# RMSNorm statistics of a two-layer hybrid block: the pre-norm's sum of squares as columns that are spread back, the post-norm's last squares added by matmul, the residual's coefficient applied on ScalarE

## The reference, cut to what matters

```
def _rmsnorm(x, g):
    y = xf * lax.rsqrt(jnp.mean(xf * xf, axis=-1, keepdims=True) + EPS)
def _pre(x, g, mod, k):
    return _rmsnorm(x, g) * (1.0 + mod[:, 3 * k + 1]) + mod[:, 3 * k]
def _post(x, y, g, mod, k, weight):
    return x + weight * mod[:, 3 * k + 2] * _rmsnorm(y, g)
```

## Time and profile before

| | |
|---|---|
| time, median of 3 runs | 2871.16 us (2861.47 to 2871.52) |
| span of the profiled execution | 2864.4 us |
| TensorE busy | 2680.7 us (94%) |
| VectorE busy | 1677.3 us (59%) |
| ScalarE busy | 716.3 us (25%) |
| mean granted TensorE clock | 0.969 |

### The profile page before, as it was taken

The page is one execution under the profiler, slowest core; times in us unless marked ns, Lnnn a source line. Parts: engine busy times, 40 slices in busy tenths (PEclk is TensorE's granted clock), DMA queues, the critical chain, the costliest instruction groups (busy, mean ns, idle before and its releaser), DMA issues.

```text
span 2864.4 us, 39514 instructions
## 1 busy us (share of the span) xinstructions
PE 2680.7 (94%) x16446; PEld 2496.0 (87%) x16446; DVE 1677.3 (59%) x2235; ACT 716.3 (25%) x977; POOL 821.0 (29%) x1292
## 2 busy tenths in 40 slices
PE   5899999998899889999999799999998898899996
PEld 4899999997869789999999699999998766588885
DVE  5868877865582686766665743343434683644444
ACT  4211121113413421111111322112122413322222
POOL 1258775732050200000000228767551050100001
PEclk9999999999999999999999899999999999899998
DMA  9443444442455134343441232222233455133321
GB/s 314 125 132 125 152 152 128 129 165 87 151 147 162 45 111 125 111 130 114 132 126 52 74 74 87 95 94 89 94 103 120 138 167 161 57 96 99 96 89 59
DMA packets 340459, 337.09 MB, mean 118 GB/s; under 512 B 52529, under 2 KB 311225, under 8 KB 336697
## 3 DMA queue, kind: packets, MB, share of 16 engines
q1 hardware_dynamic: 279224, 204.07, 24.3%
q10 hardware_dynamic: 51840, 77.07, 8.0%
q0 software_dynamic: 9216, 53.42, 5.0%
HBM read 290.02 MB, written 44.50 MB: 117 GB/s over the span
## 4 chain that ended last, share of the span: by engine, by line
PE 81%; DVE 11%; ACT 3%; DMA 2%; issue 2%; SPq 1%; POOL 0%; DVEq 0%; ACTq 0%; POOLq 0%
PE ps L454 71%; DVE adaW L541 3%; PE ps L1390 2%; PE ps L582 2%; PE ps L1089 2%; ACT wH L439 1%; PE ps L1415 1%; DVE tmpN L1168 1%; DMA y_d<-YC 1%; DVE wL L446 1%; DVE rmsX L1177 1%; DVE xT L1049 1%; PE ps L1404 1%; DMA xin<-in_x_dram 1%; PE ps L1074 1%
## 5 line engine op out<-in xcount | busy, mean ns | idle before, releaser
L454 PE MATMUL ps<-hH,wH 128*128 128x384 f32 (+1 forms) x2928 | 1019.9, 348 | 67.9 <-DVE hL L1186 48.1
L454 PE MATMUL ps<-hL,wH 128*128 128x384 f32 (+1 forms) x2928 | 1011.6, 345 | 0.0
L454 PE MATMUL ps<-hH,wL 128*128 128x384 f32 (+1 forms) x2928 | 1010.9, 345 | 0.0
L446 DVE TENSOR_TENSOR wL<-raw,wH 128x1024 fp32r<-128x1024 f32 x300 | 392.0, 1319 | 551.9 <-ACT wH L439 551.3
L454 PEld LDWEIGHTS ps<-hH,wH 128*128 128x128 f32 x2928 | 556.1, 190 | 95.6 <-issue 55.9
L454 PEld LDWEIGHTS ps<-hL,wH 128*128 128x128 f32 x2928 | 556.3, 190 | 18.1
L454 PEld LDWEIGHTS ps<-hH,wL 128*128 128x128 f32 x2928 | 555.5, 190 | 18.5
L454 PE MATMUL ps<-midH,wH 128*128 128x384 f32 (+1 forms) x1232 | 426.2, 346 | 12.7 <-DVE wL L446 9.9
L454 PE MATMUL ps<-midH,wL 128*128 128x384 f32 (+1 forms) x1232 | 423.6, 344 | 0.0
L454 PE MATMUL ps<-midL,wH 128*128 128x384 f32 (+1 forms) x1232 | 423.2, 344 | 0.0
L439 ACT ACTIVATE wH<-raw 128x1024 fp32r<-128x1024 f32 x300 | 310.8, 1050 | 448.2 <-PE ps L454 399.3
(11 more groups left out here) (257 smaller groups left out, 2382.3 us busy)
## 6 DMA issues: line engine op xcount, KB each, us to landing
raw<-in_ffn_gu_dram SPq DMA_DIRECT2D x176, 512.0 KB, 3.8
adaW<-in_w_ada_dram ACTq DMA_DIRECT2D x40, 1536.0 KB, 7.0
raw<-in_ffn_down_dram SPq DMA_DIRECT2D x88, 512.0 KB, 3.7
x_d<-xT POOLq DMA_DIRECT2D x4, 3072.0 KB, 9.6
xT<-x_d POOLq DMA_DIRECT2D x4, 3072.0 KB, 11.1
W_d<-gW POOLq DMA_DIRECT2D x16, 512.0 KB, 4.0
VT_d<-gVT ACTq DMA_DIRECT2D x16, 512.0 KB, 3.0
raw<-in_w_in_dram SPq DMA_DIRECT2D x16, 512.0 KB, 6.2
```

The costliest lines, as they stand in the source:

```text
L446: nc.vector.tensor_tensor(wL[:, n % SPLIT_SLOTS, :], raw[:, n % RAW_SLOTS, :], wH[:, n % SPLIT_SLOTS, :].bitcast(f32), ALU.subtract).then_ ...
L454: ins = nc.tensor.matmul(dst, a, b, start=first and n == 0, stop=last and n == 3 * len(pairs) - 1)
```

## The change

The pre-norm's statistic is made as the post-norm's was: `pre_tensor` takes each chunk's squares as stationary operands, six blocks of 128 tokens, against one column of ones, and accumulates over the eight chunks in six columns; ScalarE takes the root of these six columns and VectorE their reciprocal into `rstd`; TensorE waits for it (`rs_x`) and spreads the columns. `pre_vector` reads the spread from PSUM; `rmsX` is gone. This holds for the start's pre-norm too, inside `pre_tensor`.

In the post-norm chunk 7's squares go to TensorE as six more stationary blocks, instead of being added to `sumY` on VectorE. `coef_post` moves ahead of the last `down` (or of `add_half`). ScalarE multiplies `yT` by `coefP` in place, chunk m - 1 after squaring chunk m, in two instructions for the two streams; chunks 6 and 7 both come after the last square. VectorE's normalisation is then one plain multiplication of 768 tokens without a coefficient.

```
+    def stat_columns(pe, at, squares, tok0, first, last):
         for b in range(tok0 // 128, TOK // 128):
+            ins = nc.tensor.matmul(at[:, b:b + 1], squares[:, b * 128:(b + 1) * 128], ones[:, 0:1],
+                                   start=first and b == tok0 // 128, stop=last and b == TOK // 128 - 1)
+    def spread_columns(pe, tok0, place):
         for b in range(tok0 // 128, TOK // 128):
+            bank, col = place(b)
             ins = nc.tensor.matmul(ps[:, bank, col:col + 128], rstd[:, b:b + 1].broadcast_to([128, 128]), ident[:],
                                    start=True, stop=True)
     def post_tensor(pe, N, S):
-        pe.wait_ge(all_y, N.nth + 1)
-        stat_matmuls(pe, 0, N.tok0).then_inc(ss_y, 1)
+        at = ps[:, 0, 0:8]
+        pe.wait_ge(sum_y, N.nth + 1)
+        stat_columns(pe, at, sumY, N.tok0, True, False)
+        pe.wait_ge(sq_y, KC * N.nth + KC)
+        stat_columns(pe, at, sq[:, KC - 1], N.tok0, False, True).then_inc(ss_y, 1)
         pe.wait_ge(rs_y, N.nth + 1)
-        spread_matmuls(pe, 2, 3, N.tok0).then_inc(bc_y, 1)
+        spread_columns(pe, N.tok0, by_half(N.tok0)).then_inc(bc_y, 1)
     def pre_tensor(pe, N):
         for m in range(KC):
             pe.wait_ge(sq_x, KC * N.nth + m + 1)
-            for t0, t1, v in token_segments(N.tok0):
-                ins = nc.tensor.matmul(seg_ps(*N.banks, v), ones[:, 0:1].broadcast_to([128, 128]), N.sq[:, m, t0:t1],
-                                       start=m == 0, stop=m == KC - 1)
+            ins = stat_columns(pe, stat_x(N), N.sq[:, m], N.tok0, m == 0, m == KC - 1)
         ins.then_inc(ss_x, 1)
+        pe.wait_ge(rs_x, N.nth + 1)
+        spread_columns(pe, N.tok0, by_stream(N)).then_inc(bc_x, 1)
     def square_y(act, N, S, m):
         y_ready(act, S, m)
         nc.scalar.activation(sq[:, m, N.tok0:TOK], yT[:, m, N.tok0:TOK], ACT.Square).then_inc(sq_y, 1)
+        if m == 0:
+            act.wait_ge(coef_y, N.nth + 1)
+        for done in [m - 1] * (m > 0) + [m] * (m == KC - 1):
+            act.wait_ge(sq_y, KC * N.nth + done + 1)
+            for t0, t1, v in token_segments(N.tok0):
+                ins = nc.scalar.activation(yT[:, done, t0:t1], yT[:, done, t0:t1], ACT.Copy,
+                                           scale=coefP[:, done, v:v + 1])
+            ins.then_inc(y_scaled, 1)
     def pre_scalar(act, N):
-        act.wait_ge(ss_x, N.nth + 1)
-        for t0, t1, v in token_segments(N.tok0):
-            ins = nc.scalar.activation(rmsX[:, t0:t1], seg_ps(*N.banks, v), ACT.Sqrt, bias=ones[:, 1:2], scale=1.0 / D)
-        ins.then_inc(sd_x, 1)
+        root(act, stat_x(N), N.tok0, N.nth, ss_x, sd_x)
     def post_vector(dve, N, S):
-        coef_post(dve, N)
-        add_last_squares(dve, N)
...
-            for t0, t1, v in token_segments(N.tok0):
-                ins = nc.vector.scalar_tensor_tensor(tmpN[:, m % 2, t0:t1], yT[:, m, t0:t1], coefP[:, m, v:v + 1],
-                                                     seg_ps(2, 3, v), ALU.mult, ALU.mult)
-            ins.then_inc(y_norm, 1)
+            dve.wait_ge(y_scaled, KC * N.nth + m + 1)
+            nc.vector.tensor_tensor(sb_pair(tmpN[:, m % 2, :], N.tok0), sb_pair(yT[:, m, :], N.tok0),
+                                    ps_pair(1, N.tok0), ALU.mult).then_inc(y_norm, 1)
     def inverse_x(dve, N):
+        b = N.tok0 // 128
         dve.wait_ge(sd_x, N.nth + 1)
-        nc.vector.reciprocal(rmsX[:, N.tok0:TOK], rmsX[:, N.tok0:TOK]).then_inc(rs_x, 1)
+        nc.vector.reciprocal(rstd[:, b:6], sumsq[:, b:6]).then_inc(rs_x, 1)
     def pre_vector(dve, N):
-        dve.wait_ge(rs_x, N.nth + 1)
+        dve.wait_ge(bc_x, N.nth + 1)
...
-                                                     rmsX[:, t0:t1], ALU.mult, ALU.mult)
+                                                     seg_ps(*N.banks, v), ALU.mult, ALU.mult)
     def ffn_vector(dve, F, N):
...
+        coef_post(dve, N)
         down(6 * NPH - 2, 4 + 12 * (NPH - 1), NPH - 1)
     def mix_vector(dve, M, pre, N):
...
+        coef_post(dve, N)
         for m in range(KC):
             add_half(m)
```

More of the change, by code:

```diff
@@ L256, in build @@
     sq_y = sem("sq_y")
-    sum_y, all_y = sem("sum_y"), sem("all_y")
+    sum_y = sem("sum_y")
+    coef_y = sem("coef_y")
+    y_scaled = sem("y_scaled")
     ss_y = sem("ss_y")
@@ L268, in build @@
     rs_x = sem("rs_x")
+    bc_x = sem("bc_x")
     h_tmp = sem("h_tmp")
@@ L717, in ffn_scalar, with ffn_vector @@
             square_y(act, N, F, m)
-    def ffn_vector(dve, F):
+    def ffn_vector(dve, F, N):
         for m in range(KC):
@@ L1028, in add_squares @@
         ins.then_inc(sum_y, 1)
[L1030 to L1035, removed]
     POOL_CHUNKS = (1, 3, 5)
@@ L1061, in post_pool @@
             add_to_x(pool, nc.gpsimd, N, m, x_new_pool)
-    def stat_matmuls(pe, bank, tok0):
+    def stat_columns(pe, at, squares, tok0, first, last):
         for b in range(tok0 // 128, TOK // 128):
-            ins = nc.tensor.matmul(ps[:, bank, b:b + 1], sumY[:, b * 128:(b + 1) * 128], ones[:, 0:1],
-                                   start=True, stop=True)
+            ins = nc.tensor.matmul(at[:, b:b + 1], squares[:, b * 128:(b + 1) * 128], ones[:, 0:1],
+                                   start=first and b == tok0 // 128, stop=last and b == TOK // 128 - 1)
         return ins
-    def spread_matmuls(pe, bank_ctx, bank_lat, tok0):
+    def spread_columns(pe, tok0, place):
         for b in range(tok0 // 128, TOK // 128):
-            bank, col = (bank_ctx, b * 128) if b < 2 else (bank_lat, b * 128 - CTX)
+            bank, col = place(b)
             ins = nc.tensor.matmul(ps[:, bank, col:col + 128], rstd[:, b:b + 1].broadcast_to([128, 128]), ident[:],
@@ L1076, in spread_matmuls, with by_half, by_stream, stat_x @@
         return ins
+    def by_half(tok0):
+        return (lambda b: (2, b * 128 - CTX)) if tok0 else (lambda b: (2 + b // 3, b % 3 * 128))
+    def by_stream(N):
+        return lambda b: (N.banks[0], b * 128) if b < 2 else (N.banks[1], b * 128 - CTX)
     def post_tensor(pe, N, S):
-        pe.wait_ge(all_y, N.nth + 1)
-        stat_matmuls(pe, 0, N.tok0).then_inc(ss_y, 1)
+        at = ps[:, 0, 0:8]
[3 more added lines that the diff above has]
+        stat_columns(pe, at, sq[:, KC - 1], N.tok0, False, True).then_inc(ss_y, 1)
         pe.wait_ge(rs_y, N.nth + 1)
-        spread_matmuls(pe, 2, 3, N.tok0).then_inc(bc_y, 1)
+        spread_columns(pe, N.tok0, by_half(N.tok0)).then_inc(bc_y, 1)
+    def stat_x(N):
+        return ps[:, N.banks[0], 480:488]
     def pre_tensor(pe, N):
@@ L1087, in pre_tensor, with root @@
             pe.wait_ge(sq_x, KC * N.nth + m + 1)
-            for t0, t1, v in token_segments(N.tok0):
-                ins = nc.tensor.matmul(seg_ps(*N.banks, v), ones[:, 0:1].broadcast_to([128, 128]), N.sq[:, m, t0:t1],
-                                       start=m == 0, stop=m == KC - 1)
+            ins = stat_columns(pe, stat_x(N), N.sq[:, m], N.tok0, m == 0, m == KC - 1)
         ins.then_inc(ss_x, 1)
-    def root(act, bank, tok0, nth, ready, done):
+        pe.wait_ge(rs_x, N.nth + 1)
+        spread_columns(pe, N.tok0, by_stream(N)).then_inc(bc_x, 1)
+    def root(act, at, tok0, nth, ready, done):
         b = tok0 // 128
         act.wait_ge(ready, nth + 1)
-        nc.scalar.activation(sumsq[:, b:6], ps[:, bank, b:6], ACT.Sqrt, bias=ones[:, 1:2], scale=1.0 / D).then_inc(done, 1)
+        nc.scalar.activation(sumsq[:, b:6], at[:, b:6], ACT.Sqrt, bias=ones[:, 1:2], scale=1.0 / D).then_inc(done, 1)
     def square_y(act, N, S, m):
@@ L1105, in post_scalar @@
             split_hi(act, n)
-        root(act, 0, N.tok0, N.nth, ss_y, sd_y)
+        root(act, ps[:, 0, 0:8], N.tok0, N.nth, ss_y, sd_y)
     def square_x(act, N, wait_chunk):
@@ L1140, in coef_post @@
         dsync(dve)
-        dlink(dve, nc.vector.scalar_tensor_tensor(coefP[:], coefP[:], N.weight, g_chunk(N.layer, 2 * N.k + 1),
-                                                  ALU.mult, ALU.mult))
+        nc.vector.scalar_tensor_tensor(coefP[:], coefP[:], N.weight, g_chunk(N.layer, 2 * N.k + 1),
+                                       ALU.mult, ALU.mult).then_inc(coef_y, 1)
     def coef_pre(dve, N):
@@ L1162, in post_vector @@
         wait_back(dve, N)
-        dsync(dve)
         for m in range(KC):
@@ L1672, in by_chunk, with mix_vector @@
         return t[:, m, tok0:TOK].rearrange("p (c t) -> p t c", t=T8)
-    def mix_vector(dve, M, pre):
+    def mix_vector(dve, M, pre, N):
         l, tok0, c0 = M.layer, M.tok0, M.c0
@@ L2064, in _ @@
                 if kind == "ffn":
-                    ffn_vector(dve, S)
+                    ffn_vector(dve, S, N)
                 else:
-                    mix_vector(dve, S, pre)
+                    mix_vector(dve, S, pre, N)
                 post_vector(dve, N, S)
```

1 line of the change is left out of this document (removed).

## The result

| | before | after |
|---|---|---|
| median | 2869.99 us (4 runs) | 2903.35 us (4 runs, 2901.07 to 2906.38) |
| span of the profiled execution | 2864.4 us | 2904.6 us |
| mean granted TensorE clock | 0.969 | 0.947 |

The changed kernel is slower: ratio 1.0126, interval 1.0111 to 1.0142. The forecast was 2909, range 2886 to 2923. The medians differ by 33.4 us and the two profiled spans by 40.2; the sum of the prediction was 38.3. The profiled execution after is the slowest of its four.

A forecast was written before the change was run, and what follows sets the result against it. TensorE's untouched three-part products held 81% of the chain; the change touched boundaries and start. 16.5 + 7.65 + 0.9 + 11.6 + 1.95 - 0.3 = 38.3 us gave 2909 on the median, range 2886 to 2923.

The forecast's parts named there:

- The clock of the columns: Pre-norm columns on TensorE: half clock for all 96 records at boundaries; at the start, after about 3 us at full.
- The first rival: Pre-norm columns run at full clock, as TensorE streams without pause: sum -0.45 us, no change, 2871; chance 10%.
- The pre-norm's columns: Boundaries: 96 records at half clock leave a backlog, +2.9 us at each of four boundaries, +1.95 at M1.
- The loop's saving of 0.9: VectorE's loop after the post spread: plain normalisation saves 5 x 0.18 = 0.9 us at each of four boundaries.
- ScalarE's lateness: Before the post-norm's root: scaling chunks 6 and 7 delays splits, table and root, 7.65 us in all.
- The spreads: Post-norm spreads come later and take longer: +0.6 us at F1_0, 0.1 at F1_1, 0.2 at F2_1.
- F2_1's loop: VectorE's normalisation loop at F2_1, 512 tokens: saves 0.3 us.
- The half saving in VectorE's loop: VectorE's addition to xT stays held until GpSimd's ends, still 1.6 us; five of eight normalisation savings count.
- The start: First pre-norm: rides queue behind rs_x, begin 15.1 us late and at half clock; +16.5 us, bounds 12.6 to 20.
- The late rides: Rival at the start: transfers landing after 20 us instead of 12 hold ride 6 by 6 or 7 us; 2916, 7%.
- The covered start: Rival: a later wait that ends with a transfer covers the start's delay; sum 22 us, 2893; chance 5%.
- The added records in the post-norm: Post-norm column sums: twelve more records on TensorE end before ScalarE is ready.

The follow-up runs named there:

- the wide company: Changed kernel plus five unused wide one-pass matmuls after each chunk's columns, chunks 0 to 6, in the boundaries' pre-norms: 2976.63 us, ratio 1.0384.
- the post part alone: Changed post-norm, with the pre-norm and start of the kernel before: 2867.66 us, ratio 1.0003 to before.
- the pre part alone: Changed pre-norm, start included, with the post-norm of the kernel before: 2893.65 us, ratio 1.0099 to before.
- taking the start back: Changed kernel with only the start's pre-norm as before, the five boundaries left changed: 2887.98 us, ratio 1.0075 to before.

## Why the prediction was right

**The clock of the columns** was the point on which all hung, and it came as taken from the earlier trace rows: 0.50 through all columns at the boundaries, and at the start from 2.5 us on (forecast 3), with a backlog: at F2_0 they ended at 1657.49, some 9 us after VectorE's last addition to xT. The Trainium skill (TensorE: Matmul & The Clock Gate, "What's actually happening") ties the clock to how busy TensorE has lately been. The busy time in these traces does not bear that out: with 12.00 of 12.00 us busy at the start, 12.48 of 12.50 at F2_0 and 25.00 of 25.00 in the wide company the clock stayed at 0.50. The first rival, which was that rule's result, is out. Why the clock is low there stays open. That such records cost more at 0.50 is measured (2.72 us for twelve against 1.50 at 1.00).

**The pre-norm's columns.** Forecast +2.9 for each of four boundaries, measured +3.2; M1 +1.95, measured +2.4. With the last record's 0.3 us taken off, a record cost 0.214 us (20.84 over 96), as taken; the columns start 0.1 us later than forecast and end 0.25 later, which is most of the difference. The loop's saving of 0.9 exists, as the post part alone shows (24.1 to 23.2), but under the backlog only 0.36 of it counts.

**ScalarE's lateness.** Forecast 2.1, 0.5, 1.45, 2.1, 0.9 and 0.6; measured in the roots 2.01, 0.41, 1.35, 2.01, 0.73 and 0.46, 7.0 in all against 7.65. The spreads were +0.95 against +0.9. F2_1's loop saved 0.3 (10.5 us before, 10.2 after), as forecast.

**The half saving in VectorE's loop.** VectorE's and GpSimd's timeline at F2_0:

```profile
1634.76 0.96 DVE L1044 TENSOR_TENSOR xT<-xT,tmpN 128x768 f32<-128x768 f32 x1
1635.64 1.81 DVE L1178 TENSOR_TENSOR tmpN<-yT,ps 128x768 f32<-128x768 f32 x2
1637.48 1.80 DVE L1044 TENSOR_TENSOR xT<-xT,tmpN 128x768 f32<-128x768 f32 x1
```

```profile
1636.66 1.81 POOL L1044 TENSOR_TENSOR xT<-xT,tmpN 128x768 f32<-128x768 f32 x1 [11.75 <-DVE tmpN L1178]
```

The second addition is held until GpSimd's ends at 1638.47 and takes 1.80 us; in the earlier trace rows it was 1.62. The faster multiplication only made it start sooner. The multiplications at L1178, with an operand in PSUM, run beside GpSimd at their normal 0.9. The Trainium skill (GPSIMD Engine Reference, "1. Specifications") says that GpSimd shares its SBUF interface with VectorE and contends with instructions that have two SBUF inputs; the rows agree.

**The start** was the term that was mis-sized: +13.9 where I had 16.5. The columns were 0.9 us longer than forecast and everything up to the rides as described, 16.4 us late against 15.1. But I charged the rides 2.5 us for half clock, and the first two took 3.68 as before: the clock had come back at the end of the spread. The clock does not always come back there. In the pre part alone, with the same order, the row is

```profile
59.71 5.21 PE L551 MATMUL ps<-adaW,siluC 128*2 128x128 f32 x96
```

and the first product comes at 82.45. From the first ride to the first product the changed kernel takes 21.2 us, 2.4 less than before. 2.1 of these are the 1.1 of the lost wait for ScalarE, which I had counted, and a gap of 1.54 us in the last ride of the kernel before, which its profile puts down to issue, less the 0.53 us wait for a transfer. I had not counted that gap.

**The late rides.** The transfer of ride 7 did end last, by 0.53 us. The rival with a landing of 20 us did not come true. The covered start is out: taking the start back gave 15 us.

**The added records in the post-norm** cost nothing, as forecast, but only since ScalarE was later still; with the scaling moved they hold F2_0's root by 1.15 us and, with the post part alone, M1's by 1.09.

**How close the total came** is in part luck. Against the traces the start was forecast 2.6 us too large and the boundaries, with F2_1, 0.7 too small. The traces' 40.2 us hold 3.8 of scatter; against the medians, 33.4, the sum of 38.3 is 5 us too large.

## What to carry to other kernels

A statistic as one-column matmuls trades VectorE's time per token for TensorE's time per stationary load. Here such loads ran for the most part at half clock (0.21 us a record): price them so, and compare it to the pace at which the squares come. Where the columns keep up with the squares they are hidden and the small reciprocal is a gain (one-pass columns, which round the squares: 2.7 us at each boundary of 768 tokens); where they do not, the backlog takes the gain and more. Work that is put on an engine "while it waits" must be followed to the last instance, after which there is no more waiting: there it stands ahead of whatever the engine does next, and here two chunks' scaling moved behind the roots was worth 5 us by the ratios without the columns (1.0003 to 0.9987) and 9 with them (1.0126 to 1.0095).

## What the runs showed of the hardware that I had not expected

- With half of TensorE's time in wide one-pass matmuls (2.48 us of each 5.0) the clock stayed at 0.50 for 25 us. With one-pass columns and more wide matmuls ahead, one and the same sequence ran at 1.00 throughout at one boundary and fell to 0.50 at three others of one execution.
- Twelve wide one-pass matmuls right ahead of the next products: these then ran at 1.00 over their first 4 us at all five boundaries, against 0.50 to 0.65 without.
- A record of a one-pass column matmul costs as much as one of a two-record float32 matmul (2.72 us for 12 at half clock in both); what one pass saves is the number of records.
- The clock can return within or just behind a spread at the start (rides 3.68 us) or not (5.21 us), with the same instructions ahead of them.
